# Order of attention, start-up and gate work in a fused attention, mLSTM and SwiGLU layer

## The reference, cut to what matters

```
h = rms_norm(x, g_mix); p = h @ w_in
aq, ak, av, mq, mk, mv, mo, mi, mf = split(p)
att = sliding_window_attention(rms_norm(aq), rms_norm(ak), av, sinks, slopes)   # 8 heads of 64, 2 key heads
mh  = sigmoid(mo) * mlstm_chunkwise(silu(conv(mq)), silu(conv(mk)), mv, mi, mf) # 4 heads
x = x + concat(rms_norm(att), rms_norm(mh)) @ w_out
x = x + (silu(h2 @ w_gate) * (h2 @ w_up)) @ w_down                              # h2 = rms_norm(x, g_ffn)
```

## Time and profile before

| | us |
|---|---|
| median of 3 runs | 1023.62 (1022.7 to 1024.15) |
| the profiled execution, its own time | 1022.94 |
| its span, first to last instruction | 1021.1 |
| PE busy | 1005.1 (98%) |
| POOL busy | 691.5 (68%) |
| DVE busy | 646.9 (63%) |
| ACT busy | 442.5 (43%) |
| DMA, mean share of 16 engines | about 21% |

### The profile page before, as it was taken

One profiled execution on the slowest core, in us unless ns is written; L12 is line 12 of the kernel. 1 busy time (PEld: TensorE's weight loads), 2 busy tenths in 40 slices (PEclk: granted clock), 3 DMA queues, 4 the chain that ended last, 5 costly groups with the idle time before them and its releaser, 6 DMA issues.

```text
span 1021.1 us, 13479 instructions
## 1 busy us (share of the span) xinstructions
PE 1005.1 (98%) x4970; PEld 831.3 (81%) x4970; DVE 646.9 (63%) x775; ACT 442.5 (43%) x912; POOL 691.5 (68%) x543
## 2 busy tenths in 40 slices
PE   9999999999999999999999999999999999999998
PEld 7898788877877887778888888888888888888886
DVE  4259426648862579584857676574848676574585
ACT  7555135547840558433434252433434252433440
POOL 0128768826566514988778688688778688688792
PEclk9999999999999999999999999999999999999999
DMA  7213202140131002111211211211211211211213
GB/s 228 68 53 91 77 28 67 60 154 22 32 110 57 25 18 82 52 42 42 83 42 42 83 42 42 82 42 42 83 42 42 83 42 42 83 41 43 84 58 136
DMA packets 71161, 66.06 MB, mean 65 GB/s; under 512 B 5304, under 2 KB 53688, under 8 KB 71096
## 3 DMA queue, kind: packets, MB, share of 16 engines
q1 hardware_dynamic: 70104, 64.71, 20.4%
q10 hardware_dynamic: 992, 0.49, 0.2%
HBM read 60.48 MB, written 4.21 MB: 63 GB/s over the span
## 4 chain that ended last, share of the span: by engine, by line
PE 91%; DVE 4%; issue 2%; ACT 2%; POOL 1%; DMA 0%; SPq 0%; DVEq 0%; POOLq 0%; ACTq 0%
PE banks L795 29%; PE banks L797 28%; PE banks L796 28%; PE banks L815 1%; ACT prob L1489 1%; PE banks L989 1%; PE banks L886 1%; DVE af_lo L2030 1%; PE banks L964 1%; POOL wr_raw L725 0%; PE banks L898 0%; DMA w_raw<-in_w_in 0%; PE banks L953 0%; PE banks L908 0%; PE banks L862 0%
## 5 line engine op out<-in xcount | busy, mean ns | idle before, releaser
L731 POOL TENSOR_TENSOR wr_lo<-wr_raw,wr_hi 128x512 fp32r<-128x512 f32 x231 | 318.8, 1412 | 26.8 <-ACT wr_hi L1309 21.7
L725 POOL TENSOR_TENSOR wr_raw<-wr_raw,wr_raw 128x512 f32<-128x512 f32 x132 | 193.8, 1473 | 138.0 <-PE banks L797 105.9
L795 PE MATMUL banks<-hf_hi,wr_hi 128*128 128x512 f32 x616 | 240.8, 391 | 1.8 <-DVE sg L2006 1.1
L797 PE MATMUL banks<-hf_hi,wr_lo 128*128 128x512 f32 x616 | 240.4, 390 | 0.0
L796 PE MATMUL banks<-hf_lo,wr_hi 128*128 128x512 f32 x616 | 240.1, 390 | 0.0
L1309 ACT ACTIVATE wr_hi<-wr_raw 128x512 fp32r<-128x512 f32 x231 | 136.7, 625 | 158.9 <-POOL wr_raw L725 100.4
L2109 DVE TENSOR_TENSOR x<-banks,x 128x1024 f32<-128x1024 f32 x138 | 168.8, 1224 | 53.3 <-PE banks L797 39.4
L795 PE MATMUL banks<-w_hi,actT_hi 128*128 128x512 f32 (+1 forms) x448 | 173.3, 387 | 0.9 <-DVE w_lo L1700 0.9
L797 PE MATMUL banks<-w_hi,actT_lo 128*128 128x512 f32 (+1 forms) x448 | 168.2, 376 | 0.0
L796 PE MATMUL banks<-w_lo,actT_hi 128*128 128x512 f32 (+1 forms) x448 | 167.8, 375 | 0.0
L795 PEld LDWEIGHTS banks<-hf_hi,wr_hi 128*128 128x128 f32 x616 | 115.6, 188 | 27.4 <-DVE sg L2006 2.0
(11 more groups left out here) (202 smaller groups left out, 1197.0 us busy)
## 6 DMA issues: line engine op xcount, KB each, us to landing
wr_raw<-in_w_up SPq DMA_DIRECT2D x46, 256.0 KB, 3.3
wr_raw<-in_w_gate SPq DMA_DIRECT2D x44, 256.0 KB, 3.4
wr_raw<-in_w_down SPq DMA_DIRECT2D x44, 256.0 KB, 3.1
w_raw<-in_w_in SPq DMA_DIRECT2D x32, 256.0 KB, 3.5
w_raw<-in_w_out SPq DMA_DIRECT2D x16, 256.0 KB, 2.7
x<-in_x SPq DMA_DIRECT2D x8, 512.0 KB, 6.4
out<-x SPq DMA_DIRECT2D x16, 256.0 KB, 2.1
x_in<-in_x SPq DMA_DIRECT2D x7, 512.0 KB, 4.0
```

The lines of the kernel that those rows point to most:

```text
L725: nc.gpsimd.tensor_tensor(wr_raw[slot(q, f)][:, :], wr_raw[slot(q, a)][:, :], wr_raw[slot(q, b)][:, :], ALU.subtract).then_inc(wsum, 1)
L731: nc.gpsimd.tensor_tensor(wr_lo[s][:, :], wr_raw[s][:, :], wr_hi[s][:, :].bitcast(F32), ALU.subtract).then_inc(wf_lo, 1)
L795: nc.tensor.matmul(ps, x_hi, wh, start=first, stop=False, skip_group_check=more)
L797: return nc.tensor.matmul(ps, x_lo, wh, start=False, stop=last, skip_group_check=more)
```

## The change

- **Attention.** ACT no longer copies the queries out of PSUM (`aq` is gone). It makes their squares only; DVE multiplies the inverse root by the row's rstd (`qscale`, new, 128x8) and scales the queries straight from the unit's bank. So unit U waits for `qn_ready` and no longer for ACT's copy. The squares for the first tile come ahead of the mLSTM's last work on ACT (`state_squares` is moved behind) and on DVE (`query_stats(0)` at U = 32).
- DVE makes the negated largest score in one reduction, takes the smaller of it and the negated sink (`nsink`, made once at U = 0) and releases ACT's exponentials there; the sink's shift comes after.
- DVE's work for the probabilities (`probabilities`: copy of the transposed half, sum, reciprocal, multiplication) stands between the two updates of x in the units from 40 on; `query_stats` stands ahead of the penalties, the lo part of the mLSTM transposes behind `qn`.
- On ACT the squares come ahead of the mLSTM's hi part, the inverse root ahead of the work on PV.
- PE makes `att_sumsq` after `att_values`, in bank 7 and no longer in bank 3.
- **Key transposes.** They move from behind unit 18 to behind unit 19. On DVE `lf` comes ahead of the scaling of the keys, and the copies into `kT` after the cumulative maximum.
- **Start.** POOL makes the identity from `ones` with two affine_selects; ACT's queue loads `grow`; SP loads the first half of x, weight slice 0, the second half of x, then the rest. PE transposes `grow` first. `keep_warm` goes from 6 and 5 to 4 and 2. ACT and DVE treat three and four weight slices ahead of the second half's split, before two each.
- **Feed-forward seam.** In up 0 POOL makes the sum for form 4 before that for form 7, and the lo part of form 6 between them. DVE makes the lo part of form 4 in two halves with the addition of `sg[4]` between; PE waits for the second half only in the middle of the form.
- **Second gate.** DVE makes the lo part of form 3 of down 0 after the addition of `sg[4]`, no longer before it.

The core of the diff:

```diff
-            sp.dma_start(ident[:, :], consts[:, C_ID:C_ID + P]).then_inc(ident_s, 16)
...
+            pool.wait_ge(ones_set, 1)
+            nc.gpsimd.affine_select(out=ident[:, :], in_=ones[:, :], pattern=[[1, P]], compare_op=ALU.is_ge,
+                                    fill=0.0, base=0, channel_multiplier=-1).then_inc(ident_lower, 1)
+            pool.wait_ge(ident_lower, 1)
+            nc.gpsimd.affine_select(out=ident[:, :], in_=ident[:, :], pattern=[[-1, P]], compare_op=ALU.is_ge,
+                                    fill=0.0, base=0, channel_multiplier=1).then_inc(ident_set, 1)
...
                     block_sum(q, 5, 7, 5)
+                    pool.wait_ge(wsum, sum_count(q, 5))
+                    pool.wait_ge(b22_s[q % 2], n)
+                    block_sum(q, 6, 3, 5)
+                    pool.wait_ge(wsum, sum_count(q, 6))
+                    pool.wait_ge(b21_again, 16)
+                    block_sum(q, 4, 4, 6)
+                    pool.wait_ge(wsum, sum_count(q, 4))
+                    block_low(q, 6)
+                    block_sum(q, 7, 3, 7)
...
-                if U >= 2:
+                if U >= 4 * T + 2:
+                    pe.wait_ge(qn_ready, U - 4 * T - 1)
+                elif U >= 2:
                     pe.wait_ge(acc_free[U % 2], U // 2)
...
             def att_prob_transposes(t):
+                if t >= 2:
+                    pe.wait_ge(ssa_ready, t - 1)
...
                     if j == 0:
-                        pe.wait_ge(acc_free[part], UNITS // 2)
+                        pe.wait_ge(qn_ready, T - 1 + part)
...
-            keep_warm(6)
-            pe.wait_ge(ident_s, 16)
-            transpose_tile(x_in, 0, h_tp)
+            keep_warm(4)
+            pe.wait_ge(ident_set, 1)
             pe.wait_ge(gmix_s, 16)
             nc.tensor.transpose(bank[4][:, 0:K], grow[:, :], ident[0:K, 0:K]).then_inc(mix_tp, 1)
-            keep_warm(5)
+            transpose_tile(x_in, 0, h_tp)
+            keep_warm(2)
...
-                    step(nc.scalar.activation(pq[:, :], ps[:, :], ACT.Square, scale=r_))
-                    if t >= 2:
-                        act.wait_ge(qn_ready, t - 1)
-                    nc.scalar.activation(aqs[t % 2][:, :], ps[:, :], ACT.Copy, scale=r_).then_inc(free, 1)
+                    nc.scalar.activation(pq[:, :], ps[:, :], ACT.Square, scale=r_).then_inc(pq_ready, 1)
...
-                    link(V_.tensor_reduce(smx[:, :], prob[tt % 2][:, :, :], AX.X, ALU.max))
-                    link(V_.tensor_tensor(smx[:, :], smx[:, :], sink_b[:, :], ALU.max))
-                    link(V_.tensor_scalar(nmx[:, :], smx[:, :], -1.0, None, ALU.mult))
-                    V_.tensor_tensor(esk[:, :], sink_b[:, :], nmx[:, :], ALU.add).then_inc(s_max, 1)
+                    link(V_.tensor_reduce(nmx[:, :], prob[tt % 2][:, :, :], AX.X, ALU.max, negate=True))
+                    V_.tensor_tensor(nmx[:, :], nmx[:, :], nsink[:, :], ALU.min).then_inc(s_max, 1)
+                    dve.wait_ge(s_max, tt + 1)
+                    V_.tensor_tensor(esk[:, :], sink_b[:, :], nmx[:, :], ALU.add).then_inc(sink_shift, 1)
...
-                form_low(4, slice(0, 4 * P), 7)
+                form_low(4, slice(0, 4 * P), 7, slice(0, 2))
                 dve.wait_ge(copied, copy_of(0, 2))
                 add_product(sg[4], bank[4], product(0, 7))
+                form_low(4, slice(0, 4 * P), 7, slice(2, 4))
```

More of the change, by code:

```diff
@@ L164, in hymba_block @@
         qrs, _ = place("qrs", [P, 8])
+        qscale, _ = place("qscale", [P, 8])
         kss, _ = place("kss", [P, 2 * T])
@@ L916, in att_sumsq @@
                     pe.wait_ge(ssa_ready, t)
-                pe.wait_ge(mixb_ready, min(t + 4, T))
-                nc.tensor.matmul(bank[3][:, 0:1], sqb[:, 0:P], ones[:, 0:1], start=True,
+                pe.wait_ge(pTd, min(t + 2, T))
+                nc.tensor.matmul(bank[7][:, 0:1], sqb[:, 0:P], ones[:, 0:1], start=True,
                                  stop=True).then_inc(ssa_mm, 1)
@@ L1046, in _ @@
                 if U == 2 * T + 2:
-                    pe.wait_ge(kn_ready, 1)
-                    for b in range(2):
-                        for j in range(4):
-                            last = nc.tensor.transpose(bank[2 + b][:, j * P:(j + 1) * P],
-                                                       kvs[:, 4 * b + j, 2 * MH:2 * MH + KV * HD], ident[:, :])
-                    last.then_inc(kT_tp, 1)
                     pe.wait_ge(lf_ready, 1)
@@ L1060, in _ @@
                     nc.tensor.transpose(bank[6][0:32, 0:P], u_col[:, :], ident[:, :]).then_inc(uT_tp, 1)
+                    pe.wait_ge(kn_ready, 1)
+                    for b in range(2):
+                        for j in range(4):
+                            last = nc.tensor.transpose(bank[2 + b][:, j * P:(j + 1) * P],
+                                                       kvs[:, 4 * b + j, 2 * MH:2 * MH + KV * HD], ident[:, :])
+                    last.then_inc(kT_tp, 1)
                 if U == 2 * T + 4:
@@ L1329, in _ @@
             act.wait_ge(mix_ready, 1)
-            w0_high(0)
-            w0_high(1)
+            for k in range(3):
+                w0_high(k)
             high_bank(0, 1, h_tp, h_hi)
-            for k in range(2, K):
+            for k in range(3, K):
                 w0_high(k)
@@ L1710, in _ @@
             low_bank(0, 0, h_hi, h_split)
-            w0_low(0)
-            w0_low(1)
+            for k in range(4):
+                w0_low(k)
             low_bank(0, 1, h_hi, h_split)
-            for k in range(2, K):
+            for k in range(4, K):
                 w0_low(k)
@@ L1807, in _ @@
                     V_.tensor_scalar(diag[:, :], tril32, cm[:, P - 1:P], None, ALU.mult).then_inc(umax_ready, 1)
+                    dve.wait_ge(kT_tp, 1)
+                    for b in range(2):
+                        step(V_.tensor_scalar(kT[:, CHUNK + b * N:CHUNK + (b + 1) * N], bank[2 + b][:, :],
+                                              cols[:, G_K:G_K + 1], None, ALU.mult))
                 if U == 2 * T + 4:
@@ L2040, in dve_gate @@
                 add_product(sg[1], bank[5], 7 * g + 2)
+                early = len(FORMS) - (2 if j == 1 else 1)
                 if j >= 1:
-                    for f in FORMS[1:-1]:
+                    for f in FORMS[1:early]:
                         act_low(j - 1, f)
@@ L2046, in dve_gate @@
                 if j >= 1:
-                    act_low(j - 1, FORMS[-1])
+                    for f in FORMS[early:]:
+                        act_low(j - 1, f)
                 add_product(sg[2], bank[6], 7 * g + 6)
```

190 lines of the change are left out of this document (103 added, 87 removed).

## The result

The changed kernel takes 1007.05 us, the median of 4 runs (1006.74 to 1008.17); the kernel before, run beside it, 1023.88. The ratio is 0.9837 with a 95% interval of 0.9819 to 0.9854. The profiled execution took 1006.92 us with a span of 1005.2, against 1022.94 and 1021.1 before: 16.0 us less, where 11.2 were forecast. The direction was right, the size was not, and the range (down to 1009.6) missed it.

A forecast was written before the change was run, and what follows sets the result against it. PE, 98% busy, was taken as the bound. Terms summed to 9.9 us plus 1.3 for nine waits, 11.2 off 1022.94: 1011.7, with 1012.0 taken for the median; the 8-in-10 range was 1009.6 to 1015.8.

The forecast's parts named there:

- What bounds the kernel: Whole kernel: PE, busy 98% of the span, sets the end; the change can only give back PE's waits, 10.1 us listed.
- Every sign that the forecast gave for being right: PE's listed waits gone, first large product before 8 us, first PV within 0.4, feed-forward waits at most 0.4.
- none of being wrong: Signs: POOL's affine_select after 3 us, qn waits in several units, qn over 9 us late, weight-block wait at the seam.
- Keys, 1.4 and 0.15: Key transposes: PE's wait for kvs goes, lf just in time; gain 1.4 us, plus about 0.15 per wait gone.
- First queries, 1.5 and 0.15: Before attention's first tile: squares and head sums done before the mLSTM resumes; gain 1.5 us, plus about 0.15 per wait.
- PV, 4.7: Attention: first PV wait shrinks to 0 to 0.4 us, waits in units 41 to 43 go wholly; gain 4.7 us.
- bank 3, 0.5: Attention: moving the sum to bank 7, after PV, removes PE's wait; gain 0.5 us.
- queries in their bank, -0.3: Attention: queries left in their PSUM bank add waits, only unit 40 tight; cost 0.3 us, bounds 0 and 1.3.
- Feed-forward, 1.6 and 0.3: Seam and second gate: reordered sums and lo parts remove PE's waits; gain 1.6 us, plus about 0.15 per wait.
- Start, 0.5: First unit hangs on the load queue; fewer issues and bytes ahead of the fifth weight slice give 0.5 us.
- the identity is late: Start, rival: POOL's code comes at 7 us, not 1, delaying x's transposes; gain 10.1, time 1013.1 us; chance 0.17.
- fewer warming products: Start, same rival: first twelve products at lower clock, 2.4 us at most, half hidden; both together 1014.3; chance 0.17.

The follow-up runs named there:

- e1: The kernel before with 32 unused bytes per partition ahead of the large buffers, every instruction as before: 1019.18 us against 1022.42.
- e3: The changed kernel with the attention part (units 32 to 47, all engines) put back, placement kept: 1013.41 us.
- e11: The changed kernel with DVE's copy of the probabilities and their normalisation again behind the second update of x: 1011.87 us.
- e7: The changed kernel with the feed-forward orders at the seam and in the second gate put back: 1010.48 us, the change beside it 1006.96.
- e8: The changed kernel with the old start put back (identity loaded, x ahead of the weights, 6 and 5 warming rounds): 1008.53 us.
- e5: The changed kernel itself, run again with nothing altered: 1006.96 us.
- e18: The changed kernel itself once more, as partner of the run with more warming products: 1006.99 us.
- e17: The changed kernel, placement kept, with five warming rounds ahead of x and three between its halves: 1006.89 us, the change beside it 1006.99.
- e2: The changed kernel with 32 more unused bytes per partition ahead of the large buffers: 1010.76 us.
- e10: The changed kernel with only the second group of large buffers (kvs, later form buffers and upper weight slots) moved by 64 bytes: 1009.95 us.
- e16: The changed kernel with only forms 1 and 2, two upper weight slots and half of the down forms moved by 64 bytes: 1010.48 us.
- e4: The changed kernel with the keys' transposes and lf put back as they were: 1009.40 us.

## Why the prediction was right and wrong

- **What bounds the kernel:** right. Each wait that the list named came back with its part undone, in its place. Every sign that the forecast gave for being right stood in the trace (the first large product at 7.67 us, no wait of PE for kvs, qn, the sum in bank 3 or at the three feed-forward places), and none of being wrong. But none of these signs looks at the distance of one product to the next, where 2.8 us lay.
- **Keys, 1.4 and 0.15:** right, 1.7. lf was ready in time.
- **First queries, 1.5 and 0.15:** right as a sum, 1.7, wrong as a cause. The term took the wait of the earlier trace rows for the price of the order; 0.9 of it was a small step of DVE stretched beside GpSimd. The new order takes that price away too, though the step is as long as before (1.00 us); where the step is short, the same reordering gives 0.8 (e1, e3).
- **PV, 4.7, bank 3, 0.5, and queries in their bank, -0.3:** 5.4 measured, where 4.9 and 0.15 for each of five waits make 5.65. Of the first PV 0.3 is left, inside the 0 to 0.4 of the term. The three later waits went wholly, and e11 shows that putting back the copy and the normalisation alone brings them back. The cost of 0.3 in unit 40 did not appear: PE has no wait for qn anywhere.
- **Feed-forward, 1.6 and 0.3:** too small, 3.0. The step that failed is the count: the term went by idle times of about 0.3, 0.7 and 0.8 and an addition for two waits, though these are three. With the orders undone and the buffers in place (e7) the waits' idle time is 2.2, since PE comes sooner and waits 1.2 in place of 0.8, and each of the three has 0.16 on top (a large product counts as busy for 0.39 us and comes every 0.227). The rest, 0.3, is not accounted for.
- **Start, 0.5:** 0.9 between the two profiles, 0.7 between the means, and 0.4 more in the mLSTM stage, which e8 gives back too. About half of that 0.4 is scatter, since the changed kernel's own repeats (e5, e18) lose 0.2 there; whether the rest belongs to the start was not tried. Of the rival "the identity is late" nothing happened: GpSimd's first step ran at 1.17 us, 0.3 us behind the ISA row of the same line. By the Trainium skill, "GPSIMD Engine Reference", section 2.1, the first call of a freshly loaded kernel should have paid about 6 us; no run here shows it, in any of the 17 profiles with this identity. That rival's other half, fewer warming products, was real in the trace but nearly free in time (e17).
- **Placement, not in the sum:** 2.8, the largest miss, and the step that failed above all: a term put at nothing without a reason. I counted the new buffer `qscale` as an instruction's operand and not as 32 bytes that move half of the memory. The diff and the list of placements showed that large buffers were moved; nothing in the trace of before told its price, so it ought to have been an open term that widens the range on both sides. That it was a gain is luck: in the feed-forward of the changed kernel the distance of e2 costs 4.0 us and the present one nothing. Without the placement's part the range would just have held: 1007.05 and 2.8 make 1009.85, and its lower end was 1009.6.

In all, between the two profiles: start and mLSTM 1.3, keys 1.7, first queries 1.7, the rest of attention 5.4, orders of the feed-forward 3.0, placement 2.8: 15.9 of 16.0. Against the forecast's terms, placement is 2.8 of the 4.8 missed, the feed-forward 1.1, start and mLSTM 0.8.

## What to carry to other kernels

A change that adds or removes a buffer also moves all that lies behind it; before its gain is put down to the new order, run the old order with the new placement. A wait in the trace has a price and a cause apart: look whether a small step in front of the late one was stretched by a neighbour engine. That part of the wait depends on which of the two begins first, by some tens of ns, so it can come and go with any other change. Of many reorderings, look first for copies that stand behind an operation which itself waits for the end of PE's unit: one of these was worth 3.7 us in the profiles here.

## What the runs showed of the hardware

- With the two regions of buffers a multiple of 256 bytes apart, no large product between 500 and 900 us came more than 228 ns after the one before it, in any of the 13 profiles. With remainders of 32, 64, 128 and 224, 200 to 410 of the some 1760 did, at 229 to 241 ns. Most were in a quad's first three forms, and form 6's were slow also where all its own operands had stayed in place (e10, e16), so another engine's or a transfer's accesses seem to have to do with it. While slow products ran in e2, GpSimd's `wr_lo` was busy in 73% of the time, against 46% beside the others, and its `wr_raw` in none of it, against 37%. That can be the place in the quad alone; which accesses meet was not tried. The Trainium skill, "SBUF — State Buffer", section "SBUF: two separate sides", says that PE never waits on anyone there. No run here shows what holds the slow products up, so none contradicts it outright, but their pace does depend on how far other buffers lie.
- A DVE step of 4 columns took 0.16 us when it began 10 to 30 ns ahead of a GpSimd multiplication (e1, e3, e4), and 0.89 to 1.03 behind one, to that one's end (the 17 others). The step `nmx` of 8 columns took 1.22 us beside GpSimd's `w_lo` in the change.
- The table prints a granted clock of 1.00 from 0 us on, but the trace's own record of a clock of 1.00 begins only where the pace changes: at 9.6 us in the changed kernel, where the products' distance falls from 0.43 us (that of 1.2 GHz) to 0.23, and at 5.8 in the kernel before. So the 1.00 of the earlier trace rows is what the table prints where nothing is recorded, and the prediction was right to go by the durations. With 8 warming products ahead of x the record begins between 8.5 and 11.7 us, but once at 4.8, while PE stood still (e11); with 12, as before, at 4.6 to 5.8; with 10 and 6 more between x's halves, at 6.6 and 6.7.
